# Differential attention by query rows: scores once, the two maps mixed on GpSimd, one transposition and one value product

## What is computed

```python
s = jnp.einsum('bqhmd,bkhmd->bhmqk', qblk, k) * (dqk ** -0.5)     # m = 0, 1: two maps of a head
mask = key_chunk[None, :] <= q_chunk[:, None]                      # chunks of 64, causal
p = masked_softmax(s, mask)
a = (p[:, :, 0] - lam * p[:, :, 1]).astype(v.dtype)
o = jnp.einsum('bhqk,bkhd->bqhd', a, v)                            # then an RMS norm per head
```

## Time and profile before

| | us |
|---|---|
| median of three executions (2764.28 to 2766.99) | 2765.97 |
| span of the profiled execution, first to last instruction | 2765.6 |
| its attention of group C, first layer, 271.3 to 406.1 | 134.8 |
| its attention of group C, second layer, 1641 to 1776 | 135.0 |
| its attention of group A, first layer, 406.1 to 484.5 | 78.4 |

### The profile page before, as it was taken

One profiled execution on the slowest core, in us unless ns is written; L12 is line 12 of the kernel. 1 busy time (PEld: TensorE's weight loads), 2 busy tenths in 40 slices (PEclk: granted clock), 3 DMA queues, 4 the chain that ended last, 5 costly groups with the idle time before them and its releaser, 6 DMA issues.

```text
span 2765.6 us, 36226 instructions
## 1 busy us (share of the span) xinstructions
PE 2688.9 (97%) x12768; PEld 2102.4 (76%) x12768; DVE 1645.8 (60%) x3330; ACT 998.6 (36%) x2055; POOL 1262.5 (46%) x1170
## 2 busy tenths in 40 slices
PE   8999899999999999999999998999999999999997
PEld 7788467668788888888887875676787888888886
DVE  3787876635534355544959877776364534355448
ACT  2476454442222212222435654443422222212223
POOL 5433700014666556666364346001156566566661
PEclk9999899999999999999999999999999999999999
DMA  5311344523311111101152122355323101111102
GB/s 155 89 46 46 68 91 93 131 105 97 122 33 32 61 62 61 50 17 63 65 138 57 44 74 57 79 109 119 114 89 111 57 27 39 61 62 61 50 20 80
DMA packets 97418, 203.21 MB, mean 73 GB/s; under 512 B 14010, under 2 KB 23162, under 8 KB 96954
## 3 DMA queue, kind: packets, MB, share of 16 engines
q1 hardware_dynamic: 87800, 175.58, 23.5%
q10 hardware_dynamic: 9440, 25.33, 2.5%
HBM read 138.04 MB, written 8.61 MB: 53 GB/s over the span
## 4 chain that ended last, share of the span: by engine, by line
PE 87%; DVE 7%; issue 2%; DMA 2%; ACT 1%; SPq 1%; POOL 0%; ACTq 0%; DVEq 0%; POOLq 0%
PE ps L1276 8%; PE ps L1278 8%; PE ps L1277 8%; PE ps L1158 8%; PE ps L1301 7%; PE ps L1300 7%; PE ps L1302 7%; PE ps L942 4%; PE ps L943 4%; PE ps L944 4%; PE ps L1206 2%; PE ps L1208 2%; PE ps L1207 2%; PE ps L1133 1%; PE ps L1100 1%
## 5 line engine op out<-in xcount | busy, mean ns | idle before, releaser
L900 POOL TENSOR_TENSOR wlo<-wraw,whi 128x512 fp32r<-128x512 f32 (+2 forms) x336 | 444.7, 1324 | 202.1 <-ACT whi L1363 180.2
L898 POOL CAST whi<-wraw 128x512 fp32r<-128x512 f32 (+2 forms) x272 | 183.6, 675 | 740.2 <-DMA wraw<-in_w_out 289.4
L1276 PE MATMUL ps<-xhi,whi 128*128 128x512 f32 x1024 | 406.1, 397 | 0.0
L1278 PE MATMUL ps<-xhi,wlo 128*128 128x512 f32 x1024 | 405.9, 396 | 0.0
L1277 PE MATMUL ps<-xlo,whi 128*128 128x512 f32 x1024 | 405.9, 396 | 0.0
L2064 DVE TENSOR_TENSOR common<-common,ps 128x512 f32<-128x512 f32 x104 | 69.6, 687 | 460.4 <-PE ps L1302 459.9
L1301 PE MATMUL ps<-wlo,op_hi 128*128 128x512 f32 x784 | 311.7, 398 | 0.0
L1300 PE MATMUL ps<-whi,op_hi 128*128 128x512 f32 x784 | 309.5, 395 | 0.0
L1302 PE MATMUL ps<-whi,op_lo 128*128 128x512 f32 x784 | 308.0, 393 | 0.0
L1507 ACT ACTIVATE probT<-ps 128x512 f32<-128x512 f32 (+2 forms) x456 | 205.2, 457 | 240.4 <-PE ps L1142 73.8
L900 POOL TENSOR_TENSOR wlo<-down_raw,whi 128x512 fp32r<-128x512 f32 x168 | 226.2, 1349 | 98.7 <-ACT whi L1363 92.0
(11 more groups left out here) (249 smaller groups left out, 5495.4 us busy)
## 6 DMA issues: line engine op xcount, KB each, us to landing
wraw<-in_w_up SPq DMA_DIRECT2D x144, 256.0 KB, 3.1
down_raw<-in_w_down SPq DMA_DIRECT2D x112, 256.0 KB, 3.6
wraw<-in_w_in SPq DMA_DIRECT2D x80, 256.0 KB, 2.7
slot<-q_part SPq DMA_DIRECT2D x72, 256.0 KB
slot<-k_part SPq DMA_DIRECT2D x72, 256.0 KB
wraw<-in_w_out SPq DMA_DIRECT2D x64, 256.0 KB, 2.8
slot<-q_part SPq DMA_DIRECT2D x48, 128.0 KB
slot<-k_part SPq DMA_DIRECT2D x48, 128.0 KB
```

The costliest lines, as they stand in the source:

```text
L900: nc.gpsimd.tensor_tensor(lo, loaded, hi.bitcast(F32), ALU.subtract).then_inc(S["w_lo"], 1)
L1276: mm(ps[:, b, :], wh, xhi[:, k, tok], start=(k == 0), stop=False)
L1278: last = mm(ps[:, b, :], wl, xhi[:, k, tok], start=False, stop=(k == KT - 1))
```

## The change

- Group C leaves the list of jobs (`JOBS` has the 12 heads of A, B, D). It gets a loop of its own over 64 units: unit u is map u % 2 of row r = u // 2, a row being one head's tile of 128 queries, with 128 to 1024 keys. Per unit PE makes the scores once (`score_row`, two banks), DVE takes the row maximum of all keys in one instruction (`largest_row`), ACT takes the exponential with that maximum as bias and sums it (`exponent_row`).
- DVE inverts the sums of a row (`invert`), two units later. POOL mixes the two maps (`combine`): a factor on 128x1, a scaling of the second map, an addition.
- For each pair of rows PE transposes the mixed blocks (`turn_row_pair`, up to four 128x128 blocks at a time, 40 times), ACT or DVE copies them out, and PE makes one value product per head (`add_values`), transposes the result back, and DVE multiplies by the first map's inverse sum.
- POOL also takes over the preparation of A's bias and the giving back of signs. The rotary turns of C and B move from `beside_attention` to the projection, three parts at a time ahead of slabs 46 to 51 and 54 to 62; D's stay and come after the mixing.
- `find` and `select` of D's masks: the seven that ran beside C's jobs now run in `between` of A's jobs, beside the one of each kind that was there.
- Many semaphores are shared by both layers, with a count that goes on (`passed`). ACT waits for the moved turns before it splits the third part of the first pair.

```diff
-JOBS = [(hd, m) for hd in range(len(HEADS)) for m in range(2 if HEADS[hd][0] == "C" else 1)]
-C_JOBS = 2 * H
+JOBS = list(range(H, len(HEADS)))
...
+ROPE_C, ROPE_B = 46, 54
...
+PAIR_AT = {4: (0, 1), 5: (2, 1), 6: (3, 6), 7: (7, 1)}
+FIND_AT = {0: [0], 1: [2], 2: [3], 3: [4], 5: [5]}
+SELECT_AT = {0: [0], 1: [1], 2: [2], 3: [3], 4: [4], 6: [5]}
+FIND_LATE = {0: [1]}
...
+def _c_turns():
+    for g in range(C_PAIRS):
+        p = g % (TILES // 2)
+        for j in range(p + 1):
+            yield g, [(kt, i) for kt in (2 * j, 2 * j + 1) for i in (2 * p, 2 * p + 1) if kt <= i]
...
+def _c_ticks():
+    u = -1
+    for g, _ in C_TURNS:
+        u = max(u + 1, 2 * (2 * g + 1) + 1 + C_LAG)
+        yield u
...
+    return "c_taken_act" if n % 3 == 2 or C_AT[n] >= C_UNITS else "c_taken_dve"
...
+C_PAIR = {12: (1, 0), 14: (1, 1), 16: (1, 2), 18: (1, 3), 42: (2, 0), 44: (2, 1), 46: (2, 2), 48: (2, 3),
+          60: (3, 0), 62: (3, 1), 64: (3, 2), 66: (3, 3)}
...
-                if hd == 4:
-                    sp.wait_ge(S["m_row"], 16 * 7)
-                if hd == 1:
-                    sp.wait_ge(S["m_row"], 16)
-                if earlier is not None:
-                    sp.wait_ge(S["st_ready"], FIRST_STEP[max(j for j, z in enumerate(JOBS) if z[0] == earlier) + 1])
+                if earlier is not None and earlier < H:
+                    sp.wait_ge(S["c_scored"], passed(l, "c_scored") + 2 * TILES * (earlier + 1))
...
+                if n == ROPE_C:
+                    pool.wait_ge(const_loaded, 80)
+                    pool.wait_ge(S["i_acc"], NSEL * H_IDX)
+                    pool.wait_ge(S["p_out"], 8 * 3)
+                if ROPE_C <= n < ROPE_C + 6:
+                    call, stage = divmod(n - ROPE_C, 3)
+                    turn(block((C_Q, C_K)[call] + P, P), 4, cs32, DQK_C // 2, 0, TILES, (turn3, turn4), [stage])
...
+            def restore_signs():
+                pool.wait_ge(S["thr_ready"], passed(l, "thr_ready") + 1)
+                for j, c in COL.items():
+                    at_ = scores[:, SEL_AT[j]:SEL_AT[j] + SEL_N[j]]
+                    last = nc.gpsimd.tensor_scalar(at_, at_, sgn[:, c:c + 1], None, ALU.mult)
+                last.then_inc(S["signed"], 1)
...
+            def combine(r):
+                i = r % TILES
+                n = P * (i + 1)
+                first = c_rows[:, row_at(i):row_at(i) + n]
+                pool.wait_ge(S["c_inverse"], passed(l, "c_inverse") + r + 1)
+                other = second[r % 3][:, 0:n]
+                then(nc.gpsimd.tensor_scalar(ratio[:, r:r + 1], den[:, 0, r:r + 1], nlam[:, 0:1], inverse[:, 1, r:r + 1],
+                                             ALU.mult, ALU.mult))
+                then(nc.gpsimd.tensor_scalar(other, other, ratio[:, r:r + 1], None, ALU.mult))
+                nc.gpsimd.tensor_tensor(first, first, other, ALU.add).then_inc(S["c_mixed"], 1)
...
+                restore_signs()
+                for r in range(C_ROWS):
+                    combine(r)
+                    prepare_bias(r)
+                    if r == 12:
+                        pool.wait_ge(S["qk_ready"], 8)
+                        pool.wait_ge(S["c_mixed"], passed(l, "c_mixed") + r + 1)
+                        fill(stacks[2][3][HD:96, :], 0.0)
+                        nc.gpsimd.memset(stacks[2][2][HD:96, :].bitcast(F32), 0.0).then_inc(S["ones_set"], 1)
+                        pool.wait_ge(S["ones_set"], 1)
+                    if r == 24:
+                        clear_keys(0, 2)
+                clear_keys(1, 3)
...
+            def score_row(u):
+                r, m = divmod(u, 2)
+                h, i = divmod(r, TILES)
+                n = P * (i + 1)
+                if i == 0:
+                    pe.wait_ge(S["stacked_second" if m else "stacked"][SLOT[h]], stacked_count(h))
+                if u >= 2:
+                    pe.wait_ge(S["c_exp"], passed(l, "c_exp") + u - 1)
+                q, k = stacks[SLOT[h]][2 * m:2 * m + 2]
+                for c in range(0, n, W):
+                    e = min(n, c + W)
+                    last = mm(ps[:, 2 * (u % 2) + c // W, 0:e - c], q[0:SEEN, P * i:P * i + P], k[0:SEEN, c:e],
+                              start=True, stop=True)
+                last.then_inc(S["c_scored"], 1)
...
+            def turn_row_pair(n):
+                g, blocks = C_TURNS[n]
+                pe.wait_ge(S["c_mixed"], passed(l, "c_mixed") + 2 * g + 2)
+                bank = c_turn_bank(n)
+                wait_fill(c_taker(n), c_taken(n))
+                for at_, (kt, i) in enumerate(blocks):
+                    c = row_at(i) + P * kt
+                    last = nc.tensor.transpose(ps[:, bank, P * at_:P * at_ + P], c_rows[:, c:c + P], ident)
+                last.then_inc(S["c_turned"], 1)
...
+                at_ = 0
+                for kt in sorted({z[0] for z in blocks}):
+                    i0, count_ = min(i for z, i in blocks if z == kt), sum(z == kt for z, _ in blocks)
+                    o = P * (i0 - 2 * p)
+                    last = mm(ps[0:HD, 4 + g % 2, o:o + P * count_], v_c[:, kt, h, 0:HD],
+                              probT[n % 4][:, P * at_:P * (at_ + count_)], start=kt == 0, stop=kt == 2 * p + 1)
+                    at_ += count_
+                last.then_inc(S["c_added"], 1)
...
+            for u in range(C_END):
+                if u < C_UNITS:
+                    score_row(u)
+                for p in first_pieces_at(u):
+                    score(0, p)
+                if u in C_TICK:
+                    turn_row_pair(C_TICK[u])
+                if u in C_PAIR:
+                    p, j = C_PAIR[u]
+                    wait_fill("qk_lo", 4 * p + j + 1)
+                    turn_qk(p, j, c_bank(c_fill("qk_lo", 4 * p + j + 1)))
+                if u - 2 in C_TICK:
+                    add_values(C_TICK[u - 2])
+                for g in c_outputs_at(u):
+                    turn_back(g)
+                if u == C_MAX_TURN:
+                    turn_max(0)
...
+            def exponent_row(u):
+                r, m = divmod(u, 2)
+                h, i = divmod(r, TILES)
+                n, g = P * (i + 1), r // 2
+                act.wait_ge(S["c_max"], passed(l, "c_max") + u + 1)
+                if m == 0 and h:
+                    act.wait_ge(S["c_turned"], passed(l, "c_turned") + C_LAST[g - TILES // 2] + 1)
+                if m and r >= 3:
+                    act.wait_ge(S["c_mixed"], passed(l, "c_mixed") + r - 2)
+                dst = second[r % 3][:, 0:n] if m else c_rows[:, row_at(i):row_at(i) + n]
+                nc.scalar.activation(dst, ps[:, 2 * (u % 2):2 * (u % 2) + 2, :].rearrange("p b n -> p (b n)")[:, 0:n],
+                                     ACT.Exp, bias=nmc[:, u:u + 1], scale=SCALE["C"],
+                                     accum_out=den[:, m, r:r + 1]).then_inc(S["c_exp"], 1)
...
-            act.wait_ge(S["thr_ready"], 1)
-            for j, c in COL.items():
-                seg = scores[:, SEL_AT[j]:SEL_AT[j] + SEL_N[j]]
-                last = nc.scalar.activation(seg, seg, ACT.Copy, scale=sgn[:, c:c + 1])
-            last.then_inc(S["signed"], 1)
...
+                for j in FIND_AT.get(job, []) if job == 0 else []:
+                    find(j)
+                for j in SELECT_AT.get(job, []):
+                    select(j)
+                for j in FIND_LATE.get(job, []) if job == 0 else FIND_AT.get(job, []):
+                    find(j)
+                if job in (1, 2):
+                    square_c(4 * (job - 1))
...
+            def largest_row(u):
+                r, m = divmod(u, 2)
+                n = P * (r % TILES + 1)
+                dve.wait_ge(S["c_scored"], passed(l, "c_scored") + u + 1)
+                if u >= 2:
+                    dve.wait_ge(S["c_max"], passed(l, "c_max") + u - 1)
+                v_.tensor_tensor_reduce(
+                    out=junk_c[u % 2][:, 0:n], in0=ps[:, 2 * (u % 2):2 * (u % 2) + 2, :].rearrange("p b n -> p (b n)")[:, 0:n],
+                    in1=zero[:, 0:1].broadcast_to((P, n)), scale=-SCALE["C"], scalar=3e38,
+                    op0=ALU.add, op1=ALU.min, accum_out=nmc[:, u:u + 1]).then_inc(S["c_max"], 1)
...
+            def invert(r):
+                dve.wait_ge(S["c_exp"], passed(l, "c_exp") + 2 * r + 2)
+                v_.reciprocal(inverse[:, :, r], den[:, :, r]).then_inc(S["c_inverse"], 1)
...
+                    largest_row(u)
+                if u >= 3 and u % 2 and u // 2 <= C_ROWS:
+                    invert(u // 2 - 1)
```

More of the change, by code:

```diff
@@ L332, in _steps @@
 def _steps():
-    for job, (hd, _) in enumerate(JOBS):
+    for job, hd in enumerate(JOBS):
         kind = HEADS[hd][0]
@@ new lines, in c_taken, with _c_fills, c_fill, c_bank @@
+def c_taken(n):
+    return sum(c_taker(z) == c_taker(n) for z in range(n + 1))
+def _c_fills():
+    for u in range(C_END):
+        if u in C_TICK:
+            yield u, c_taker(C_TICK[u]), c_taken(C_TICK[u])
+        if u in C_PAIR:
+            p, j = C_PAIR[u]
```

(20 more changed lines are left out.)

423 lines of the change are left out of this document (270 added, 153 removed).

## The result

The changed kernel takes 2905.23 us (2898.82 to 2909.67) where the kernel before took 2765.72 in runs on the same chip: ratio 1.0501, 95% interval 1.0486 to 1.0516, slower. 2750 was forecast and 2793 was the upper end; the prediction was wrong. The profiled execution took 2903.17, its span is 2901.0.

What follows compares the result with a forecast made beforehand. In C PE was held to wait in order for ACT and DVE; after, POOL longest (99 us). Per layer 18 won, less 4 (clock) and 6 (A's gaps): 8, twice 16, so 2765.6 - 16 = 2750 us, range 2720 to 2793.

Steps and rivals of the forecast that it cites:

- POOL's scaling (24 us, 0.13 + 0.00105 n): In C, POOL's scaling of the second map by a per-partition factor, priced by the cast's mean: 24 us per layer.
- Rival 2: POOL's scaling in C costs as much as its addition: -14 us per layer, 2794 us, slower; chance 0.18.
- I go pair by pair ... 24.3 per head: C's time summed over a head's four row pairs, POOL's mixing against the other engines' loop: 24.3 us, 97 for four heads.
- twelve splits and six comparisons 3: In C, the twelve splits and six comparisons were to add 3 us to the first layer's time.
- one pair and a tail: End of C: a last pair of 7.7 us, then transpositions, copies, A's first maxima and a DMA, 8 us.
- The longer counts: In C, POOL mixes one pair while the loop does the next; only the longer of the two adds time.
- The turns of C and B ... Hidden: 0: Turns moved to POOL in the projection, 2.7 us ahead of a slab, cost 0; without POOL's lead 6 us.
- A's gaps (6 us; 0 to 14): Seven `find` and `select` moved into A's gaps on DVE cost 6 us per layer, between 0 and 14.
- What is above 5.4 counts: Of DVE's gaps in A, only the part over 5.4 us reaches PE: 1.1 + 1.8 + 2.7 us.
- The clock (4 us): PE's granted clock in C has more low stretches: 4 us per layer lost, between 0 and 19.
- Rival 3: PE stays at 1.2 GHz through C: -7 us per layer, 2780 us; chance 0.14.
- 18 us won in C: First layer: A's first step at about 388 us instead of 406.1, 18 us won per layer before clock losses.

Runs made afterwards that it cites:

- the mix on VectorE: The changed kernel with VectorE instead of GpSimd mixing each row, by one instruction after its inverse; 2855.1 us, ratio 1.0316 to the kernel before.
- the filler: Four useless TensorE products ahead of each group of transposed rows, on the changed kernel without GpSimd's scaling (2879.2 us) or with VectorE mixing each row (2902.4 us).
- short maxima: The changed kernel without GpSimd's scaling and factor, each maximum of C taken over its row's first 128 columns only; 2802.2 us, ratio 1.0130.
- the run with the changed tail: The changed kernel with VectorE mixing, rows transposed two units earlier, turns of A's second pair earlier, the six comparisons later; 2859.5 us, ratio 1.0336.
- half and half run: The changed kernel with VectorE mixing the odd rows by one instruction each and GpSimd the even rows; 2872.8 us, ratio 1.0382.

## Why the prediction was wrong

- **POOL's scaling (24 us, 0.13 + 0.00105 n).** This step failed first. It was priced from the cast because both have one tensor input; it cost 55.2. Rival 2's deciding point, 0.89 us for 512 columns, was passed by far: 1.57. Even the upper bound, the addition's 1.26, was too low. The signs, by the same price, cost 12.1 instead of 5.3. Leaving scaling and factor out gives 28 to 38 us per layer back. Put into the prediction's own sum pair by pair, the measured rows make a head 30.5 us instead of 24.3 and, with the signs, C some 149 instead of 117 (an estimate from POOL's groups above). The other 24 to 30 of the measured 173 and 179 are no price of POOL's.
- **"I go pair by pair ... 24.3 per head", 97.** Without the scaling the first two heads take 27 each, near to it, as POOL and the loop run side by side. But "twelve splits and six comparisons 3" looks too little (the third head takes 33.7), and the end was taken as one pair and a tail, some 16 us, where 36 pass: nine groups of transposed blocks (seven of them through one bank), four splits and A's first pieces lie in it. Shortening that end only moved the time. For the rest the forecast had only half of a score, a maximum, an exponential and a hand-over per unit, and nothing beside them for waits in program order: 29 us less of VectorE's maxima gave 14. How much of it each side task adds stays open; changing who copies, when the splits come and how C ends changed C by 0 to 4 us. That leaves 142 to 145 where 117 were forecast, with POOL's scaling at nothing: a second miss, nearly as large as the first, whose cause is not isolated.
- **"The longer counts".** POOL was to be full and the rest to hide behind it. It was idle for 15.7 us (18.8 in the second layer) for the inverses. The likely reason, which no run isolates: `invert` stands two units behind the exponential in DVE's order, and DVE in turn waits for PE, which waits for POOL.
- **"The turns of C and B ... Hidden: 0".** Only POOL's lead was looked at, and PE does not wait for it there. The turns hold VectorE's small instructions in the search, which nothing covers: 10 and 12 us by the run without them, the whole delay of C's start. The trace of before had shown it. The scaling of 256 columns by VectorE takes 1.28 and 1.16 us while POOL turns, 0.34 and 0.28 afterwards, in the kernel before:

```profile
309.52 1.28 DVE L1806 TENSOR_SCALAR bias_a<-bias_a,far 128x256 f32<-128x256 f32 x1
...
310.91 1.16 DVE L1806 TENSOR_SCALAR bias_a<-bias_a,far 128x256 f32<-128x256 f32 x1
...
342.35 0.34 DVE L1806 TENSOR_SCALAR bias_a<-bias_a,far 128x256 f32<-128x256 f32 x1
...
342.80 0.28 DVE L1806 TENSOR_SCALAR bias_a<-bias_a,far 128x256 f32<-128x256 f32 x1
```

  The Trainium skill, page "SBUF — State Buffer", section "Who interferes with whom", has the rule: VectorE and GpSimd share a port pair under an exclusive lock; a VectorE instruction with two SBUF inputs, or in a two-port mode, waits for a GpSimd instruction that reads SBUF to end. The search agrees with it (28 instructions that end with GpSimd's, compares that are not touched), and so do the maxima of C (0.69 us for 512 columns in both kernels). Beside GpSimd's scaling the traces show less than the rule: in the mix on VectorE a ratio took 0.77 us instead of 0.22 beside a scaling of 1024 columns, but ended 1.7 us before it did.
- **A's gaps (6 us; 0 to 14).** The mechanism was right, the size too small: 14.3 and 18.5, of which spreading the searches gave back 5.5 and 8.8; PE's idle time there rose from 6.2 us to 17.2 and 18.5. "What is above 5.4 counts" gave 1.8 for a block that measured 7.33 us and left 4.73 idle; the 1.2 GHz behind each gap comes on top (granted clock 0.66 from 510 to 520).
- **The clock (4 us).** It fell to 0.79 and 0.74, below the 0.85 to 0.9 that was to be seen. How much of C it costs was not isolated: where TensorE's work was changed, the clock was higher with more work (0.84 to 0.89 with the filler) and lower with less (0.84 to 0.71 and 0.66), and the two effects on the time can't be told apart. Rival 3 stays open in its size.
- **Right:** DVE 86, ACT 74 and the addition's 45 us; SP's copies, D's turns and ACT's new wait, none of which shows up as a wait of weight.

The forecast's sign hung on 18 us won in C. Net of the clock it was -14 per layer and came out at +38 and +44.

## What to carry to other kernels

Price an instruction by a row of the same operation and operands, not of the same number of inputs; where there is none, the range must reach beyond the dearest neighbour. Before work is moved to GpSimd, look at what VectorE does at that moment and whether anything covers it: the two are not independent, and a row that takes four times its usual time in the old trace is the sign. In a loop of several engines in program order the longest engine's sum is a lower bound, not the time; here, from short maxima to the run with the changed tail, 86 to 119 us of the busiest of VectorE, ScalarE and GpSimd made 128 to 157 us of stage.

## What the runs showed of the hardware

- GpSimd's multiplication by a per-partition factor takes 1.57 us for 128x512 (2.84 for 1024), its two-input addition 1.27 and its cast 0.61; with a single column and two factors it takes 0.334.
- A VectorE instruction of six elements per partition (0.17 us) takes up to 1.28 us if it starts while GpSimd is in a two-input instruction of 512 columns, and up to 0.41 beside the end of a cast: all 28 delayed ones in the search end 0.02 to 0.03 us after GpSimd's. In the half and half run the 128x1 ratio took 2.02 us instead of 0.22 beside an addition of 896 columns, and ended 0.02 us after it.
- GpSimd can be the one that is late: its addition of 896 columns took 2.70 us instead of 2.08 beside a mix of VectorE's.
- TensorE's granted clock in C was lower with less work (0.87 to 0.72 and 0.88 to 0.74 with half of its turns and values, where C itself stayed at 130 us and the time rose by 8).
